# Masked attention heads: both score tiles first, then both mask tiles, and a later wait for the sparse mask

## What is computed

```python
# layer 0, heads of kind A: window of 128 keys, and a sink in the softmax
mask = (diff >= 0) & (diff < A_WINDOW) & (kpos >= 0)
s = jnp.where(mask, s, -jnp.inf)
# layer 0, heads of kind B: the n_top best keys of each query by an index score
_, idx = lax.top_k(score, n_top)
s = jnp.where(valid, einsum(q, k[idx]) * scale, -jnp.inf)
# layer 1: 16 causal heads (one block of 256 keys, so plain causal attention)
s = jnp.where(kpos <= tpos, s, -jnp.inf)
p = jax.nn.softmax(s); o = einsum(p, v)
```

## Time and profile before

| what | value |
|---|---|
| time, median of 3 runs | 1023.18 us (1022.13 to 1024.34) |
| the profiled execution, its own time | 1021.59 us |
| its span in the trace | 1019.8 us |
| TensorE products busy | 964.0 us, 95% |
| TensorE weight loads busy | 779.8 us, 76% |
| DVE, ACT, POOL busy | 713.6, 545.0, 49.5 us |
| transfers | 204.85 MB, mean 201 GB/s |

### The profile page before, as it was taken

How to read it: one execution, slowest core, us unless ns; L and a number is a source line. 1 busy time by engine, 2 the same in 40 slices (tenths; PEclk the granted TensorE clock), 3 DMA queues, 4 the chain that set the end, 5 groups by cost and what they waited for, 6 DMA issues and landing times.

```text
span 1019.8 us, 14658 instructions
## 1 busy us (share of the span) xinstructions
PE 964.0 (95%) x5676; PEld 779.8 (76%) x5676; DVE 713.6 (70%) x1061; ACT 545.0 (53%) x873; POOL 49.5 (5%) x39
## 2 busy tenths in 40 slices
PE   6986989999999999999899999999999999999995
PEld 3763657989898877777798989877888887876684
DVE  3588657877778886667875544578555778797775
ACT  3357734654455363655565445435556656656672
POOL 0000001500000000000250100000000000000000
PEclk9999999999999999999999999999999999999998
DMA  9847476979899587432788865655434355551151
GB/s 349 276 141 301 166 247 189 297 278 324 314 312 319 188 298 253 143 99 84 240 286 241 245 200 177 205 165 171 158 100 151 96 167 191 194 168 63 32 166 41
DMA packets 106931, 204.85 MB, mean 201 GB/s; under 512 B 3488, under 2 KB 37680, under 8 KB 106864
## 3 DMA queue, kind: packets, MB, share of 16 engines
q1 hardware_dynamic: 103808, 193.26, 56.1%
q0 software_dynamic: 3056, 10.67, 3.6%
HBM read 202.76 MB, written 1.15 MB: 200 GB/s over the span
## 4 chain that ended last, share of the span: by engine, by line
PE 74%; DVE 11%; ACT 6%; DMA 5%; issue 3%; SPq 1%; ACTq 0%; DVEq 0%
PE bank L1728 15%; PE bank L1731 15%; PE bank L1734 15%; PE bank L1795 5%; PE bank L1789 5%; PE bank L1792 5%; PE bank L1814 3%; DVE w_lo L1918 3%; PE bank L1836 2%; PE bank L1622 1%; DMA raw<-in_ada_w 1%; DMA raw<-in_mlp_w 1%; PE bank L1866 1%; ACT w_hi L1329 1%; DMA tok<-in_ada_w 1%
## 5 line engine op out<-in xcount | busy, mean ns | idle before, releaser
L1918 DVE TENSOR_TENSOR w_lo<-raw,w_hi 128x2048 fp32r<-128x2048 f32 (+2 forms) x134 | 309.8, 2320 | 145.5 <-ACT w_hi L1329 144.2
L1329 ACT ACTIVATE w_hi<-raw 128x2048 fp32r<-128x2048 f32 (+2 forms) x134 | 248.6, 1858 | 134.2 <-PE bank L1734 63.9
L1728 PE MATMUL bank<-w_hi,ht_hi 128*128 128x512 f32 (+1 forms) x528 | 145.9, 398 | 3.1 <-ACT full L1393 1.9
L1731 PE MATMUL bank<-w_lo,ht_hi 128*128 128x512 f32 (+1 forms) x544 | 145.9, 390 | 0.7 <-DVE w_lo L1918 0.7
L1734 PE MATMUL bank<-w_hi,ht_lo 128*128 128x512 f32 (+1 forms) x528 | 139.7, 386 | 0.0
L1731 PEld LDWEIGHTS bank<-w_lo,ht_hi 128*128 128x128 f32 x544 | 101.9, 189 | 23.5 <-DVE w_lo L1918 1.9
L1728 PEld LDWEIGHTS bank<-w_hi,ht_hi 128*128 128x128 f32 x528 | 94.8, 189 | 27.7 <-issue 8.4
L1734 PEld LDWEIGHTS bank<-w_hi,ht_lo 128*128 128x128 f32 x528 | 98.5, 188 | 20.6
L1731 PE MATMUL bank<-w_lo,hid_hi 128*128 128x512 f32 x256 | 68.5, 389 | 0.0
L1728 PE MATMUL bank<-w_hi,hid_hi 128*128 128x512 f32 x240 | 65.6, 395 | 0.0
L1734 PE MATMUL bank<-w_hi,hid_lo 128*128 128x512 f32 x240 | 64.2, 389 | 0.0
(11 more groups left out here) (253 smaller groups left out, 1261.2 us busy)
## 6 DMA issues: line engine op xcount, KB each, us to landing
raw<-in_mlp_w SPq DMA_DIRECT2D x64, 1024.0 KB, 6.6
raw<-in_ada_w SPq DMA_DIRECT2D x44, 1024.0 KB, 5.2
raw<-in_a_w_in SPq DMA_DIRECT2D x16, 1024.0 KB, 5.2
raw<-in_c_w_in SPq DMA_DIRECT2D x12, 1024.0 KB, 5.8
raw<-in_b_w_in SPq DMA_DIRECT2D x10, 1024.0 KB, 5.1
raw<-in_ple_w_gate SPq DMA_DIRECT2D x8, 1024.0 KB, 5.0
raw<-in_ab_w_in SPq DMA_DIRECT2D x4, 1024.0 KB, 9.9
tok<-in_ada_w SPq DMA_DIRECT2D x4, 1024.0 KB, 12.8
```

The costliest lines, as they stand in the source:

```text
L1329: nc.scalar.activation(split_parts(n)[0], raw_tile(t), ACT.Copy).then_inc(high_done, 1)
L1728: nc.tensor.matmul(dst, a_hi[:, first + k, rows], hi[:, k, :], start=it["first"] and k == 0, stop=False)
L1731: nc.tensor.matmul(dst, a_hi[:, first + k, rows], lo[:, k, :], start=False, stop=False)
L1918: nc.vector.tensor_tensor(lo, raw_tile(split[n]), hi.bitcast(F32), ALU.subtract).then_inc(low_done, 1)
```

## The change

In `scores` the loop over the token tiles now holds the score products alone. After it comes, for the sparse kind, the wait for `mask_ready`, which stood ahead of the first score product before. Then a second loop over the token tiles holds the mask products. The number of products, their sizes, operands and places in PSUM stay as they were. For the masked kinds `start` is now set on the score product of tile 0 alone and `stop` on the mask product of tile 1 alone: one accumulation for the whole bank. The semaphores are set by the same two instructions as before, the mask products of tile 1. The steps `index`, near and full are built as before.

```diff
                     enter(it["after"])
                     enter(it["banks"])
-                    if mode == "sparse":
-                        pe.wait_ge(mask_ready, 1)
+                    masked = mode in ("causal", "window", "sparse")
                     for t in range(T):
                         m = head_cols(mode, t)
-                        masks = {"causal": [(t * P, maskb[:, 2, :])],
-                                 "window": [(0, maskb[:, 2 - t:3, :].rearrange("p a n -> p (a n)"))],
-                                 "sparse": [(0, smask[:, t, 0:m])]}.get(mode, [])
                         done = []
                         for j in range(2):
                             qc, half, kc = it["heads"][j][0:3]
                             part = slice(half * HD, (half + 1) * HD)
                             b, _ = it["banks"][j]
                             done.append(nc.tensor.matmul(bank[b][:, t * S:t * S + m], qkt[part, qc, t * P:(t + 1) * P],
-                                                         qkt[part, kc, 0:m], start=True, stop=not masks))
-                        for j in range(2):
-                            b, _ = it["banks"][j]
-                            for o, mask in masks:
-                                done[j] = nc.tensor.matmul(bank[b][:, t * S + o:t * S + m], maskb[:, 0, :], mask, start=False, stop=True)
+                                                         qkt[part, kc, 0:m], start=t == 0 or not masked, stop=not masked))
+                    if mode == "sparse":
+                        pe.wait_ge(mask_ready, 1)
+                    if masked:
+                        for t in range(T):
+                            m = head_cols(mode, t)
+                            o, mask = {"causal": (t * P, maskb[:, 2, :]),
+                                       "window": (0, maskb[:, 2 - t:3, :].rearrange("p a n -> p (a n)")),
+                                       "sparse": (0, smask[:, t, 0:m])}[mode]
+                            for j in range(2):
+                                b, _ = it["banks"][j]
+                                done[j] = nc.tensor.matmul(bank[b][:, t * S + o:t * S + m], maskb[:, 0, :], mask, start=False, stop=t == T - 1)
                     for mm in done:
                         mm.then_inc(index_scores if mode == "index" else scores_ready, 1)
```

## The result

In five executions on one chip the changed kernel took 1018.09 us (median, 1017.35 to 1019.03) and the kernel before 1023.18 us (1022.13 to 1024.34). The ratio is 0.995, with a 95% interval of 0.9939 to 0.9962: 5.1 us less. The forecast was 1019.7 us and 3.5 us less, with a range from 1018.2. The direction and the mechanism in the pairs came out as written.

A forecast was written before the change was run, and what follows sets the result against it. TensorE, busy 95% of the span, was taken as the bound where it has no gaps. Window 0.29, sparse 0.87 and causal 2.32 us sum to 3.5 us, taking 1023.18 to 1019.7 us, range 1018.2 to 1021.9.

The forecast's parts named there:

- The length of a pair: TensorE's masked pairs: window 1.59 to 1.30 us, causal 1.49 to 1.19; 0.29 us taken a pair.
- The distance that no row showed: Last mask product of tile 0 to first of tile 1: between 0.06 and 0.15 us, taken as 0.06.
- rival (a): The four masks do not stream: 0.20 us gained a pair, 1020.8 us; chance 0.10.
- Rival (b): Weight loads wait wherever rows are shared: pair stays 1.59 us, kernel 1023.2 us; chance 0.06.
- two prices: In a masked pair, splitting the scores by a mask block costs 0.19 us, changing from mask to score 0.09 us.
- Which pairs count: On the path: window pair 0, sparse pairs 4, 5, 7 and eight causal pairs; 12 x 0.29 = 3.5 us.
- The wait at nothing: Moving the sparse pairs' wait for `mask_ready` behind the scores brings 0; it was satisfied 1.3 us before TensorE came.
- Carried whole to the end: After the pairs, everything is started by TensorE's products, so the 3.5 us gain reaches the kernel's end whole.
- Rival (c): Behind the attention, transfers or DVE's weight work take gain back: 1020.9 us, or 1022.0 if causal too; chance 0.11.
- Rival (d): Longer idle between window pairs brings half-clock stretches, 1.7 us lost each; four give 1026.5 us; chance 0.03.
- How the numbers follow: Closing step weighing forecast (0.70) and rivals into 1018.2 to 1021.9 us; faster by over 0.2% 0.83, slower 0.03.
- the spread of three runs: Basis of the forecast's own range, 1.1 us either side of 1019.7: runs from 1022.13 to 1024.34 us.

The follow-up runs named there:

- masks-apart kernel: Against the kernel before: tile 0's masks first, then all scores, then tile 1's masks; 1020.7 us, ratio 0.9978.
- the other sets' medians: The changed kernel unaltered, executed again in two later sets against the kernel before; 1018.57 us (ratio 0.9962) and 1018.99 us (0.9969).
- the fill: Unused products put where TensorE waits, in the kernel before (1024.2 us, ratio 1.0011) and in the changed kernel (1020.46 us, ratio 0.9975).

## Why the prediction was right, and where it was not

**The length of a pair** was right: 1.30 and 1.19 us forecast, 1.29 and 1.18 seen, and 0.30 us less a pair where 0.29 was forecast. The distance that no row showed, from the second mask product to the third, was taken as 0.06 us and is 0.056. With it rival (a) falls, whose distance was 0.15. Rival (b), no overlap, falls too: pairs are 0.3 us shorter. What the Trainium skill (TensorE: Matmul & The Clock Gate, Part 3, The mechanism) states, that weight loads overlap only when the row group differs, does not agree with these rows: four mask products on all rows start 0.056 to 0.109 us apart. The prediction's two prices, 0.19 us for splitting the scores and 0.09 for a change from masks to scores, hold as well, with one addition: the masks-apart kernel shows that the 0.09 us go with the change into the score rows, wherever it stands, and not with keeping the masks together.

**Which pairs count** was right. Pair 0 is passed on: it starts 0.06 us later than before and the values behind it, at 100.54, start 0.22 us earlier. The gain of pairs 1 to 3 becomes idle time, 0.31 us each (1.01 to 1.32 us ahead of the pair at 87.18). Pairs 4, 5 and 7 count, pair 6 is absorbed (idle 0.15 to 0.53 us, "about 0.4" forecast), and the gain at 133 us is 1.06 us, forecast 1.16. The causal stage gives 2.37 us, forecast 2.32, through the gap of 0.46 us that moves with them. The kernels with one half of the change confirm the two sums apart, 1.20 ± 0.61 and 2.21 ± 0.61.

**The wait at nothing** was right, by the kernel that puts it back: its sparse pair takes the same 1.29 us.

**Carried whole to the end** was right in that nothing was taken back. The transfer forecast for about 132.0 us starts at 132.14:

```profile
132.14 0.37 SPq L1227 DMA_DIRECT2D raw<-in_ab_w_out  x1
```

Rival (c), gain taken back behind the attention, falls: the distance grew there instead, by 0.71 and 0.33 us. Rival (d), slower by more half-clock stretches, falls: the three profiled executions of the kernel after have one stretch fewer than the kernel before has in both of its own, three against four.

**What was wrong**, the step that failed, is the size given to everything outside the pairs. The prediction put it at nothing ("I carry it whole to the end") and let a range of 1.1 us to either side, in the step "How the numbers follow", cover the rest. In the profiled execution it was 0.8 us, and in the medians of the first comparison 1.6.

First, the clock. It entered the sum as 0, the range as "one clock stretch more or less", and the rivals only as a loss, in (d), with the idle time between window pairs as its cause. The rows on which it rested show a stretch at half clock that follows TensorE's idle time; that there is one at 152.1 us too does not appear, because the page's slices of 25 us show nothing of a stretch of 3.4 us. Its absence brought 0.71 us in the profiled execution. The weight tiles brought 0.33 us there, which later executions did not keep, and the half-clock stretch near 930 us took 0.26 back.

Second, the range took "the spread of three runs" for the scatter of a median. But the three runs said little: over 97 executions the kernel before spread from 1020.8 to 1027.1 us, with 0.51 us for each 0.001 of mean clock. The choice of executions alone made about 1 us of the first comparison: 5.1 us there, 4.1 us between the means of all runs, 3.95 ± 0.45 at equal clock. With the other sets' medians, 1018.57 and 1018.99, the time lies inside the range. With 1 us for these executions and 1 us for the clock on the gaining side, the low end would have been 1019.7 - 2.0 = 1017.7, below the 1018.09 measured. That the first median fell outside while two later ones fall inside is in part the luck of the executions.

What stays open: whether the 0.45 us by which the kernel after exceeds the pairs' sum at equal clock is real. The interval holds zero. Open too is whether the order of the kernel after makes the stretch near 152 us rarer: the fill meant to isolate the clock ran on the path, and how often each kernel meets that stretch was not measured.

## What to carry to other kernels

Price a reordering by the distances between starts of neighbouring instructions in the timeline, with the same work elsewhere in the kernel as the yardstick for what a clean stream costs; it was right here to 0.02 us a pair. Count the changes between 64-row and 128-row work from the work in front of the block to the work behind it, not from the block's first instruction: read the short way, the masks-apart order seemed to give up a third of the gain, and it gave up 0.02 us a pair. Then walk along the path and strike off the pairs behind which TensorE waits anyway. For gains of a third of a per cent, look for every stretch at half clock first (the page's slices are too coarse), allow it on both sides, and compare executions at equal mean clock, with enough of them: five are not enough.

## What the runs showed that I had not expected

- The mean granted clock of an execution goes with more than half of the scatter, 0.51 us for each 0.001; fitted kernel by kernel, the slope lies between 0.3 and 0.65. Two kernels with half the change looked like 0.9 and 0.2 us by their medians and are 2.2 and 1.2 us at equal clock.
- Much the same idle time near 149 us, 1.75 to 2.06 us in all eleven profiled executions without filling, had no stretch at half clock behind it in five, one in four and a double one in two. In the first comparison 1.45 us of products were lost behind it before, and none after.
- All four masks of a pair together are worth 0.02 us more than two and two. Nearly the whole gain is in entering the score rows once instead of twice.
- Products added to raise the clock raised it (0.997 in the profiled execution, 0.992 in the mean, against 0.989) and still cost 2.4 us, since they had to wait for a bank that came free only 1 us before the useful work could start.
